# Expert rows gathered as two 4 KB halves from two tables, each half refilled by its own reader

## The chip, the cores and the metric

The kernel runs on one core of a Trainium2 chip. The metric is the device time of one execution in microseconds, the median of several runs. One profiled execution supplies the trace.

## The reference, cut to what matters

The model is a two-layer transformer-like block followed by a second block. The change touches only the last stage of the second block, a product-key expert layer over 256 tokens in two blocks of 128. For each token and each of 8 heads, 16 of 16384 experts are selected; an expert has a row of `u_tab` and a row of `v_tab`, each 1024 float32 (4 KB):

```
eidx = take_along_axis(cidx, pos)                       # 128 tokens x 8 heads x 16 experts
gates = softmax(best)
act = gelu(einsum('td,thkd->thk', hb, u_tab[eidx]))     # dot of each token with its expert's u row
out = einsum('thk,thkd->td', gates * act, v_tab[eidx])  # weighted sum of the v rows
```

So 2 x 8 x 16 = 256 steps each take one u row and one v row for each of 128 tokens.

## The kernel before, in words

The stage is the function `peer` (from L3004). Tokens lie on the 128 partitions. A step `e` (0 to 255) handles one of the 16 experts of one of the 8 heads of one token block; a unit is the 16 steps of one head, so there are 16 units.

The host packs each expert's u row and v row side by side in one table `experts` of 8 KB rows. GpSimd (POOL) issues one indirect DMA a step (L3164), which fetches one 8 KB row for each partition, 1 MB in all, into slot `e % 8` of a ring of 8 slots (`fetched`, L3039). Four slots lie in the `work` buffer and four in `weight_ring`, which is why each operation of the trace has two names. `urows` and `vrows` (L3040) are the two halves of a slot.

What a step does, by engine:

- POOL waits until the slot is free and issues the gather. The first four need no slot wait; those of steps 4 to 7 wait for the query products that used `weight_ring`; from step 8 on POOL waits for `product`, PE's count of finished steps (L3161). At the first step of each unit it waits also for `ranked` (L3159), the count of units whose expert numbers are found.
- VectorE (DVE) waits for the gather's semaphore and multiplies the u half by the tokens with a running sum (L3187). It writes the product back over the u half, and counts `vec_out`. Between the steps it does a slice of the search for later units' experts (the class `Search`: L3066 to L3140).
- ScalarE (ACT) applies Gelu (L3276), multiplies by the gate (L3278), and scales an identity matrix by the result (L3282), which it counts in `act_out`.
- PE waits for `act_out` and for the gather, and runs two 512-column products of that diagonal matrix with the v half, accumulated in PSUM (L3382). Its last one counts `product`. In the first four units PE also runs a query product (L3319) in each step.

POOL's instructions run in program order, so a wait holds everything behind it. All 256 gathers are issued by POOL and run on one queue, q0 in the trace. SP issues four loads of query weights at the start and two stores at the ends of the token blocks.

Of the kernel before, what the change touches and what calls it, by code (L numbers as in the profile page):

```python
# [51 lines left out]
PEER_RING = 8  # L52
# [60 lines left out]
class Core:  # L113


    def __init__(self, nc, ctx):
# [24 lines left out]
        def sem(name):  # L141
            return ctx.enter_context(nc.semaphore(name))
# [136 lines left out]
        self.fetched = False  # L279

        self.gathered = [sem(f"gathered{i}") for i in range(PEER_RING)]

        self.constants_loaded = sem("constants_loaded")
        self.rows_loaded = sem("rows_loaded")
# [2719 lines left out]
def peer(c, a, out_rows):  # L3004
# [10 lines left out]
    experts_u = experts.bitcast(U32)  # L3015
# [136 lines left out]
    with c.stage() as block:  # L3152
        units = [(u, u // H) for u in range(2 * H)]

        @block.gpsimd
        def _(pool):
            for e in range(2 * H * K):
                if e % K == 0:
                    pool.wait_ge(c.ranked, e // K + 1)  # L3159
                if e >= R:  # L3160
                    pool.wait_ge(c.product, e - R + 1)  # L3161
                elif e >= R // 2:
                    pool.wait_ge(c.queried, e - R // 2 + 1)
                pool.indirect_dma_start(  # L3164
                    out=fetched[e % R], out_offset=None, in_=a["experts"],
                    in_offset=bass.IndirectOffsetOnAxis(ap=experts_u[:, e:e + 1], axis=0)
                ).then_inc(c.gathered[e % R], 16)

        @block.vector
        def _(dve):  # L3170
# [135 lines left out]
        @block.tensor  # L3306
        def _(pe):
            def weights(n):
                if n < len(PEER_EARLY):
                    pe.wait_ge(c.ahead[n], 16 * had[n])  # L3310
                    return c.ring[:, n]
                pe.wait_ge(c.late_loaded[n - len(PEER_EARLY)], 16)
                return late_slots[n - len(PEER_EARLY)]

            def query_product(n, i, k):

                if i == 0 and k == 0 and n >= 2:
                    pe.wait_ge(c.query_copied, n - 1)
                last = pe.matmul(query_bank(n)[:, i * NLAT:(i + 1) * NLAT], weights(n)[:, k, i * P:(i + 1) * P], hs[:, k, :],  # L3319
                                 start=k == 0, stop=k == KT - 1)  # L3320
                if i == 1 and k == KT - 1:
                    last.then_inc(c.queried, 1)

            def query(n):
                for i in range(2):
                    for k in range(KT):
                        query_product(n, i, k)

            def score(n):
                pe.wait_ge(c.query_copied, n + 1)  # L3330
                if n == 0:
                    pe.wait_ge(c.side_loaded, 16)
                if n >= 2:
                    pe.wait_ge(c.score_copied, n - 1)
                for t in range(2):
                    for i in range(2):
                        last = pe.matmul(score_bank(n)[:, (2 * t + i) * P:(2 * t + i + 1) * P],  # L3337
                                         qh[:, 2 * queried[n] + i, t * P:(t + 1) * P], keys[:, i, :], start=True, stop=True)
                last.then_inc(c.scored, 1)

            def turn_tokens(t):
                for r in (2 * t, 2 * t + 1):
                    for i in range(4):
                        k = 4 * (r % 2) + i
                        last = pe.transpose(c.banks[r][:, i * P:(i + 1) * P], hs[:, k, t * P:(t + 1) * P], c.constant("ident"))  # L3345
                    last.then_inc(c.token_turned, 1)

            def turn_rows(n):

                if n == 0:  # L3350
                    pe.wait_ge(c.score_copied, 2 * H // 2)
                if n >= 4:
                    pe.wait_ge(c.row_copied, n - 3)
                for i in range(4):
                    k = 4 * (n % 2) + i
                    if n < 4:
                        source = c.x[:, k, NCTX + n // 2 * P:NCTX + (n // 2 + 1) * P]
                    else:
                        column = c.mod[:, 5 * KT + k, 0:1] if n < 6 else c.vector("final_norm", k, k + 1)
                        source = column.to_broadcast([P, P])  # L3360
                    last = pe.transpose(c.banks[4 + n % 4][:, i * P:(i + 1) * P], source, c.constant("ident"))  # L3361
                last.then_inc(c.row_turned, 1)

            query(0)
            turn_tokens(0)
            score(0)
            turn_tokens(1)
            query(1)
            query(2)
            score(1)  # L3370
            query(3)
            score(2)
            score(3)
            pe.wait_ge(c.token_copied, 4)

            for u, t in units:
                for at in range(K):
                    e, r = u * K + at, at % R
                    pe.wait_ge(c.act_out, e + 1)
                    pe.wait_ge(c.gathered[r], 16 * (e // R + 1))  # L3380
                    for half in range(2):
                        last = pe.matmul(c.banks[2 * t + half][:], diag[:, r, :], vrows[r][:, half * 512:(half + 1) * 512],  # L3382
                                         start=e == t * H * K, stop=e == (t + 1) * H * K - 1)
                    last.then_inc(c.product, 1)
                    if u < len(PEER_LATE):
                        query_product(len(PEER_EARLY) + u, at // KT, at % KT)
                    if 0 <= u - 1 < len(PEER_LATE) and at == 5:
                        score(len(PEER_EARLY) + u - 1)
                    if u == PEER_ROWS_UNIT and at < 8:
                        turn_rows(at)  # L3390
# [20 lines left out]
STREAMED = ("w_in", "w_br_ml", "w_br_da", "w_br_fn", "w_out", "w_ffn_in", "w_ffn_out", "w_in_2", "w_out_2",  # L3411
            "s5_glu_w_2", "peer_wq_2")

PACKED = ("vectors", "lambdas", "w_ada_first", "condition_rows", "ada_turned", "constants", "residual", "s5_b", "s5_c", "s5_bt", "s5_rows", "keys", "experts")
OUT = (NLAT, D)


# [91 lines left out]
def pack_inputs(x):  # L3509
    tokens = np.concatenate([x["ctx"][0], x["x"][0]], 0)  # L3510
    m = {name: np.ascontiguousarray(x[name]) for name in STREAMED}
    by_slot = np.arange(D).reshape(FN_GROUPS, FN_C)
    by_slot = np.concatenate([by_slot[:, 0:P + 1], by_slot[:, :P:-1]], 1).reshape(-1)
    m["w_br_fn"] = np.ascontiguousarray(x["w_br_fn"][:, by_slot, :])
    m["vectors"] = pack_vectors(x)
    m["lambdas"] = np.ascontiguousarray(np.broadcast_to(x["da_lam"].reshape(1, -1), (P, 2 * 4 * DA_DH)))
    m["w_ada_first"] = np.ascontiguousarray(x["w_ada"][0][:, 0:START_TILES * P].reshape(KT, P, -1, CHUNK).transpose(2, 1, 0, 3))
    m["condition_rows"] = np.ascontiguousarray(np.stack([x["c_ctx"].reshape(-1), x["c"].reshape(-1), x["c_2"].reshape(-1)]))
    wide = np.stack([x["w_ada"][0], x["w_ada"][1], x["ada_w_2"][0]])
    m["ada_turned"] = np.ascontiguousarray(wide.reshape(3, D, 48, P).transpose(0, 3, 2, 1))  # L3520
    m["constants"] = pack_constants()
    m["residual"] = np.ascontiguousarray(tokens.T.reshape(KT, P, T).transpose(1, 0, 2))

    b = np.zeros((2, P, 4, P), np.float32)
    cc = np.zeros((2, P, S5_TILES, 2 * S5_H), np.float32)
    bt = np.zeros((2, P, S5_TILES, 2 * S5_H), np.float32)
    for part, (bn, cn) in enumerate((("s5_b_re_2", "s5_c_re_2"), ("s5_b_im_2", "s5_c_im_2"))):
        for g in range(S5_G):
            i, second = g // 2, g % 2
            row = 2 * S5_H * (i % 4) + S5_H * second  # L3530
            b[part, row:row + S5_H, i // 4, S5_P * second:S5_P * (second + 1)] = x[bn][0, g].T
            tile = S5_ORDER.index(i)
            cc[part, S5_P * second:S5_P * (second + 1), tile, S5_H * second:S5_H * (second + 1)] = x[cn][0, g].T
            bt[part, S5_P * second:S5_P * (second + 1), tile, S5_H * second:S5_H * (second + 1)] = x[bn][0, g]
    m["s5_b"], m["s5_c"], m["s5_bt"] = b.transpose(1, 0, 2, 3).reshape(P, 4, 2 * P).copy(), cc, bt
    by_tile = np.stack([value.reshape(4, 4, P) for _, value in s5_parameters(x)])
    m["s5_rows"] = np.ascontiguousarray(np.repeat(by_tile.transpose(0, 2, 1, 3), 2 * S5_H, 1).reshape(3, P, 4 * P))
    m["experts"] = np.concatenate([x["peer_u_2"][0], x["peer_v_2"][0]], 1)
    m["keys"] = np.ascontiguousarray(np.stack([x["peer_keys1_2"][0].T, x["peer_keys2_2"][0].T], 1))
    return m  # L3540

# [14 lines left out]
```

## Time and profile before

| What | Value |
|---|---|
| median of 3 runs | 3282.04 us (3276.58 to 3290.23) |
| profiled execution | 3289.03 us |
| its span, first to last instruction | 3287.2 us |
| mean granted TensorE clock | 0.983 |
| PE, DVE, ACT, POOL busy, share of the span | 93%, 50%, 23%, 10% |
| queue q0 (issued by POOL) | 51936 packets, 343.17 MB |

The shares are averages over all stages. The expert stage is the last fifth of the span. "Idle before" in a row is the time that the engine stood before those instructions, with what ended it; a DMA-issuing instruction of POOL is shown with the time that it took to write its descriptors, not with the transfer's.

### The profile page before, as it was taken

Reading aid. Unit: us, or ns where it says so; the run is one execution under the profiler, and the core shown is the slowest. Engines: PE = TensorE matmul, PEld = TensorE weight load, DVE = VectorE, ACT = ScalarE, POOL = GpSimd, SP = SyncE. Lnnn points to the kernel's source line nnn. Section 1 sums busy time; section 2 is a strip of 40 time slices with the busy share of each in tenths; the row PEclk is TensorE's granted clock in tenths of the full one; section 3 lists DMA queues with packets and bytes.
Section 4 is the critical chain, followed back from the end, with each engine's and each line's share of the span. In section 5 each row is a group of like instructions: output and inputs, shape, how many; then the busy total and the mean of one; then the engine's idle time right before and its main releaser. Section 6 shows DMA issues by size and latency. Waiting matters only on the chain. (4 is left out here: it accounts for less than half of the span.)

```text
span 3287.2 us, 33311 instructions
## 1 busy us (share of the span) xinstructions
PE 3066.1 (93%) x12426; PEld 2126.5 (65%) x12426; DVE 1657.1 (50%) x3666; ACT 766.9 (23%) x1785; POOL 335.8 (10%) x371
## 2 busy tenths in 40 slices
PE   6999999999999999999999999999989899877776
PEld 2556556758888888486776678878877744322222
DVE  4333444356773666313234457553037377777774
ACT  2122133321002100012112330010023244444443
POOL 0000000000000000100000000000000144444432
PEclk9999999999999999999999999999988999999999
DMA  6211111144441544642222234577331599999997
GB/s 233 84 62 60 52 52 52 54 145 135 127 131 63 156 152 131 203 146 78 90 81 73 62 102 154 189 279 268 128 122 53 169 417 420 421 420 421 420 420 305
DMA packets 280767, 585.87 MB, mean 178 GB/s; under 512 B 11736, under 2 KB 231768, under 8 KB 244256
## 3 DMA queue, kind: packets, MB, share of 16 engines
q0 software_dynamic: 51936, 343.17, 26.5%
q1 hardware_dynamic: 228672, 240.58, 22.7%
q8 instruction: 100, 1.64, 0.2%
q14 instruction: 59, 0.48, 0.0%
HBM read 582.63 MB, written 1.08 MB: 178 GB/s over the span
## 5 line engine op out<-in xcount | busy, mean ns | idle before, releaser
L782 PE MATMUL banks<-normed,weight_ring 128*128 128x512 f32 (+1 forms) x1280 | 484.1, 533 | 18.4 <-PEq L308 18.4
L782 PEld LDWEIGHTS banks<-normed,weight_ring 128*128 128x128 f32 x1280 | 243.0, 191 | 238.1 <-issue 227.1
L791 PE MATMUL banks<-weight_ring,normed 128*128 128x256 f32 x1408 | 321.5, 384 | 0.2 <-DVE work L1274 0.2
L3382 PE MATMUL banks<-weight_ring,work 128*128 128x512 f32 x512 | 250.0, 615 | 59.1 <-ACT work L3282 58.1
L3382 PE MATMUL banks<-work 128*128 128x512 f32 x512 | 253.4, 618 | 53.6 <-ACT work L3282 49.7
L791 PEld LDWEIGHTS banks<-weight_ring,normed 128*128 128x128 f32 x1408 | 266.4, 191 | 55.6 <-issue 20.0
L417 DVE CUSTOM_DVE_ANT_0 work<-work 128x1024 f32<-128x1024 f32 x188 | 223.2, 1223 | 125.9 <-DMA work<-ada_turned 107.1
L2046 PE MATMUL banks<-normed,weight_ring 128*128 128x256 f32 x1088 | 242.7, 386 | 11.6 <-DMA weight_ring<-w_ffn_in 5.0
L2046 PEld LDWEIGHTS banks<-normed,weight_ring 128*128 128x128 f32 x1088 | 210.7, 194 | 43.1 <-DMA weight_ring<-w_ffn_in 6.3
L3382 PEld LDWEIGHTS banks<-weight_ring,work 128*128 128x128 f32 x512 | 89.0, 190 | 199.2 <-ACT work L3282 133.9
L3382 PEld LDWEIGHTS banks<-work 128*128 128x128 f32 x512 | 88.6, 190 | 197.8 <-ACT work L3282 131.9
L1583 PE MATMUL banks<-branches,weight_ring 128*128 128x256 f32 (+1 forms) x656 | 207.5, 478 | 3.4 <-PEq L308 3.4
L3187 DVE CUSTOM_DVE_ANT_0 work<-work,branches 128x1024 f32<-128x1024 f32 x128 | 156.8, 1225 | 96.3 <-DMA work<-experts,branches 96.0
L3187 DVE CUSTOM_DVE_ANT_0 weight_ring<-weight_ring,branches 128x1024 f32<-128x1024 f32 x128 | 156.8, 1225 | 89.1 <-DMA weight_ring<-experts,branches 87.4
L1583 PEld LDWEIGHTS banks<-branches,weight_ring 128*128 128x128 f32 x656 | 124.6, 190 | 84.6 <-issue 75.5
L1607 PE MATMUL banks<-work 128*128 128x256 f32 x744 | 165.6, 379 | 0.0
L3164 POOL DMA_INDIRECT work<-experts,branches x128 | 135.0, 1055 | 243.8 <-PE banks L3382 171.4
L2046 PE MATMUL banks<-branches,weight_ring 128*128 128x256 f32 x736 | 159.8, 379 | 0.0
L3164 POOL DMA_INDIRECT weight_ring<-experts,branches x128 | 140.0, 1094 | 181.6 <-PE banks L3382 175.0
L1607 PEld LDWEIGHTS banks<-work 128*128 128x128 f32 x744 | 141.4, 190 | 19.2
L2046 PEld LDWEIGHTS banks<-branches,weight_ring 128*128 128x128 f32 x736 | 139.8, 190 | 19.0
L388 POOL DMA_DIRECT2D work<-ada_turned x98 | 51.8, 529 | 768.3 <-DVEq L423 768.3
(492 smaller groups left out, 3929.5 us busy)
## 6 DMA issues: line engine op xcount, KB each, us to landing
weight_ring<-w_in SPq DMA_DIRECT2D x98, 1024.0 KB, 5.2
weight_ring<-w_ffn_in SPq DMA_DIRECT2D x44, 1024.0 KB, 5.2
work<-ada_turned POOLq DMA_DIRECT2D x80, 512.0 KB, 3.8
work<-ada_turned POOLq DMA_DIRECT2D x18, 1536.0 KB, 9.1
weight_ring<-w_ffn_out SPq DMA_DIRECT2D x20, 1024.0 KB, 5.1
weight_ring<-w_out SPq DMA_DIRECT2D x12, 1024.0 KB, 5.2
weight_ring<-w_br_ml SPq DMA_DIRECT2D x8, 1024.0 KB, 5.2
weight_ring<-w_br_da SPq DMA_DIRECT2D x8, 1024.0 KB, 5.2
```

The source lines that it names most:

```text
L388: pool.dma_start(self.slots[n % ADA_SLOTS][:, 0:nt, :], self.a["ada_turned"][which, :, t0:t0 + nt, :]).then_inc(c.ada_loaded[n % ADA_SLOTS ...
L417: last = dve.tensor_tensor_reduce(out=out, in0=slot[:, t, :], in1=self.rows[:, row, :], scale=1.0, scalar=0.0, op0=ALU.mult, op1=ALU.add, ...
L782: last = pe.matmul(proj_bank(tile)[:, since:T], w[:, kk, half * P:(half + 1) * P], c.h[:, kk, since:T], start=kk == 0, stop=kk == KT - 1)
L791: last = pe.matmul(proj_bank(tile)[:, x * CHUNK:(x + 1) * CHUNK], c.h[:, kk, j * P:(j + 1) * P], w[:, kk, :], start=kk == 0, stop=kk == KT ...
L1583: ins = pe.matmul(bank(i)[:, cols(p0, p1)], w[:, k - at, half * P:(half + 1) * P], source[:, k, cols(p0, p1)], start=k == 0, stop=k == tot ...
L1607: last = pe.matmul(out[:, half * NCTX:(half + 1) * NCTX], left(k), right(k), start=k == 0, stop=k == KT // 2 - 1)
L2046: ins = pe.matmul(bank(i)[:, 0:NLAT], w[:, k - at, half * P:(half + 1) * P], source[:, k, lat], start=k == 0, stop=k == total - 1)
L3164: pool.indirect_dma_start(out=fetched[e % R], out_offset=None, in_=a["experts"], in_offset=bass.IndirectOffsetOnAxis(ap=experts_u[:, e:e + ...
L3187: dve.tensor_tensor_reduce(out=urows[e % R], in0=urows[e % R], in1=tokens[:, t, :], scale=1.0, scalar=0.0, op0=ALU.mult, op1=ALU.add, accu ...
L3382: last = pe.matmul(c.banks[2 * t + half][:], diag[:, r, :], vrows[r][:, half * 512:(half + 1) * 512], start=e == t * H * K, stop=e == (t + ...
```

## The change

The table is split in two, `experts_in` (u rows) and `experts_out` (v rows), with 4 KB rows. A step now has two gathers of 128 rows of 4 KB, 0.5 MB each, with semaphores of their own. The u gather waits for `vec_out`: DVE is done with the u half of the step 8 before. The v gather behind it waits for `product`: PE is done with that step's v half. DVE waits for the first semaphore, PE for the second. Slots, ring depth, DVE's, ACT's and PE's instructions stay.

```diff
         self.gathered = [sem(f"gathered{i}") for i in range(PEER_RING)]
+        self.gathered_out = [sem(f"gathered_out{i}") for i in range(PEER_RING)]
...
                 if e >= R:
-                    pool.wait_ge(c.product, e - R + 1)
+                    pool.wait_ge(c.vec_out, e - R + 1)
                 elif e >= R // 2:
                     pool.wait_ge(c.queried, e - R // 2 + 1)
                 pool.indirect_dma_start(
-                    out=fetched[e % R], out_offset=None, in_=a["experts"],
+                    out=urows[e % R], out_offset=None, in_=a["experts_in"],
                     in_offset=bass.IndirectOffsetOnAxis(ap=experts_u[:, e:e + 1], axis=0)
                 ).then_inc(c.gathered[e % R], 16)
+                if e >= R:
+                    pool.wait_ge(c.product, e - R + 1)
+                pool.indirect_dma_start(
+                    out=vrows[e % R], out_offset=None, in_=a["experts_out"],
+                    in_offset=bass.IndirectOffsetOnAxis(ap=experts_u[:, e:e + 1], axis=0)
+                ).then_inc(c.gathered_out[e % R], 16)
...
                     pe.wait_ge(c.act_out, e + 1)
-                    pe.wait_ge(c.gathered[r], 16 * (e // R + 1))
+                    pe.wait_ge(c.gathered_out[r], 16 * (e // R + 1))
...
-    m["experts"] = np.concatenate([x["peer_u_2"][0], x["peer_v_2"][0]], 1)
+    m["experts_in"] = np.ascontiguousarray(x["peer_u_2"][0])
+    m["experts_out"] = np.ascontiguousarray(x["peer_v_2"][0])
```

## Rows read from the trace of the kernel before

**Rows 1.** Busy time and count by engine, granted clock, DMA share, GB/s, by stretch.

```profile
core 0: us, PE busy (x) PEld busy (x) DVE busy (x) ACT busy (x) POOL busy (x), PEclk, DMA share, GB/s
2600.00:2700.00 100.00, 95.73 (x345) 61.58 (x344) 70.91 (x208) 40.09 (x106) 42.40 (x36) 0.98 0.91 363
2900.00:3000.00 100.00, 76.40 (x157) 26.60 (x156) 74.47 (x186) 44.43 (x128) 42.09 (x39) 1.00 1.01 421
2619.40:3267.40 648.00, 536.87 (x1272) 219.22 (x1271) 452.43 (x1148) 286.46 (x833) 275.07 (x256) 0.99 1.00 415
```

**Rows 2.** The chain that ended last, its last pieces: start us, us, what.

```profile
3236.02 15.21 DMA weight_ring<-experts,branches
...
3255.90 16.17 DMA weight_ring<-experts,branches
...
3274.49 2.00 PE banks L3382 x4
```

**Rows 3.** DMA queues from 2800 to 3200 us: packets, MB, share.

```profile
q0 software_dynamic: 22993, 167.45, 100.8%
q1 hardware_dynamic: 144, 0.52, 0.3%
```

**Rows 4.** POOL in order of time at the stage's start: start us, us, instruction, idle before.

```profile
2619.41 1.01 POOL L3164 DMA_INDIRECT work<-experts,branches  x1 [63.07 <-DVEq L3131]
2620.73 0.95 POOL L3164 DMA_INDIRECT work<-experts,branches  x1 [0.30 <-issue]
...
2625.72 0.94 POOL L3164 DMA_INDIRECT weight_ring<-experts,branches  x1 [0.30 <-issue]
2626.97 0.93 POOL L3164 DMA_INDIRECT weight_ring<-experts,branches  x1 [0.31 <-issue]
```

**Rows 5.** The gathers' line alone: minimum, median, maximum ns; first and last start.

```profile
L3164 POOL DMA_INDIRECT work<-experts,branches x128: 932/936/1967, 2619.4 to 3245.9; - x128
L3164 POOL DMA_INDIRECT weight_ring<-experts,branches x128: 932/937/1991, 2624.5 to 3255.9; - x128
```

**Rows 6.** Groups by line, from 2600 us on: count, busy us, mean ns, idle before.

```profile
L3187 DVE CUSTOM_DVE_ANT_0 work<-work,branches 128x1024 f32<-128x1024 f32 x128 | 156.8, 1225 | 96.3 <-DMA work<-experts,branches 96.0 <-DVE work L3114 0.2
L3164 POOL DMA_INDIRECT weight_ring<-experts,branches x128 | 140.0, 1094 | 181.6 <-PE banks L3382 175.0 <-issue 4.0 <-PE banks L3319 2.7
L3164 POOL DMA_INDIRECT work<-experts,branches x128 | 135.0, 1055 | 243.8 <-PE banks L3382 171.4 <-DVEq L3131 63.1 <-issue 9.4
```

**Rows 7.** DVE, POOL and others in order of time, around 2886 and 2907 us.

```profile
2886.24 1.23 DVE L3187 CUSTOM_DVE_ANT_0 weight_ring<-weight_ring,branches 128x1024 f32<-128x1024 f32 x1 [1.24 <-DMA weight_ring<-experts,branches]
2886.37 1.91 POOL L3164 DMA_INDIRECT weight_ring<-experts,branches  x1 [0.57 <-PE banks L3382]
2887.40 0.08 DVE L3187 DVE_READ_ACCUMULATOR2_ANT work<- 128x1 f32 x1
...
2906.73 0.94 POOL L3164 DMA_INDIRECT weight_ring<-experts,branches  x1 [1.59 <-PE banks L3382]
2907.14 1.22 DVE L3187 CUSTOM_DVE_ANT_0 weight_ring<-weight_ring,branches 128x1024 f32<-128x1024 f32 x1 [0.86 <-DMA weight_ring<-experts,branches]
```

**Rows 8.** DMA issues: count, KB each, median us from issue to landing.

```profile
work<-ada_turned POOLq DMA_DIRECT2D x80, 512.0 KB, 3.8
work<-ada_turned POOLq DMA_DIRECT2D x18, 1536.0 KB, 9.1
```

**Rows 9.** The line that issues those loads: minimum, median, maximum ns.

```profile
L388 POOL DMA_DIRECT2D work<-ada_turned x98: 528/528/567, 2.0 to 2247.3; - x98
```

**Rows 10.** The DMA view from 2600 to 2610 us: only loads with 1 KB rows.

```profile
DMA packets 3496, 3.53 MB, mean 353 GB/s; under 512 B 48, under 2 KB 3496, under 8 KB 3496
q1 hardware_dynamic: 3496, 3.53, 109.3%
```

**Rows 11.** Around the last step, in order of time.

```profile
3272.20 1.23 DVE L3187 CUSTOM_DVE_ANT_0 weight_ring<-weight_ring,branches 128x1024 f32<-128x1024 f32 x1 [1.25 <-DMA weight_ring<-experts,branches]
...
3274.49 1.98 PE L3382 MATMUL banks<-weight_ring,work 128*128 128x512 f32 x4 [0.50 <-ACT work L3282]
```

More of the change, by code:

```diff
@@ L3412 @@
             "s5_glu_w_2", "peer_wq_2")
-PACKED = ("vectors", "lambdas", "w_ada_first", "condition_rows", "ada_turned", "constants", "residual", "s5_b", "s5_c", "s5_bt", "s5_rows", "keys", "experts")
+PACKED = ("vectors", "lambdas", "w_ada_first", "condition_rows", "ada_turned", "constants", "residual", "s5_b", "s5_c", "s5_bt", "s5_rows", "keys", "experts_in", "experts_out")
 OUT = (NLAT, D)
```

## The prediction

> **What bounds the kernel now.** I read the stretches first. In the expert stage the DMA share is 1.01 at 421 GB/s, while PE is busy 76 us of 100, DVE 74 and POOL 42 [rows 1]. The chain of waits agrees: its last fifth is made of gathers of 15 to 16 us each with a few microseconds of compute between them, down to the last gather, issued at 3255.90 and landed at 3272.07 [rows 2]. A gather that needs 15 us stands in line behind six others. The queue view says the same: q0 alone takes 100.8% of the 16 engines' time [rows 3]. So a step costs what 1 MB costs on the DMA engines: 1.0486 MB / 421 GB/s = 2.49 us, and 256 steps 638 us of the 648 us between the first issue and the end of the transfers [rows 1]. PE (two products) and DVE (one L3187 of 1.225 us [rows 6] and a slice of search) both wait in each step. POOL has one gather a step and spends the rest waiting for PE: of its idle time before gathers, 175.0 + 171.4 us were ended by PE's products [rows 6].
>
> **What the change takes away.** It lets the u half be refilled when DVE is done with it instead of when PE is, about 3 to 4 us earlier (DVE's end at 3273.4 and PE's at 3276.5 in the last step [rows 11]). With the DMA engines full, an earlier request only waits longer in the queue: the bytes are the same, so this is worth nothing in the steady state. It is also partly undone by POOL's order, since the u gather stands behind the previous step's v gather and its wait for `product`. At the end something is won: the last u half lands one half gather (1.24 us, below) before the last v half, so DVE and ACT (3272.20 to 3274.49 [rows 11]) run partly beside that transfer. Gain 1.2 us.
>
> **What it adds on POOL.** 256 more gathers, 512 in all. The price of one is its descriptor writing, 0.936 us in the median [rows 5], plus 0.30 us to the next where nothing is waited for [rows 4]. Together 1.24 us, and the starts 2625.72 and 2626.97, with a satisfied wait between them, show the same 1.25. Does a row of half the length make it cheaper? Direct loads from POOL come with 4 KB rows (512 KB) and 12 KB rows (1536 KB) [rows 8], and all 98 take 528 to 567 ns [rows 9]. So the row count sets it, and 128 rows stay 128 rows. Bounds: 0.47 us (half of the median) if it went by bytes, 0.94 if by rows; I take 0.94. A step then needs 2 x 1.24 = 2.48 us of POOL against 2.49 us of DMA. POOL, which had half its time free, has none left.
>
> **The second term: starts that are held back.** The mean of a gather is not 0.936 but (140.0 + 135.0)/256 = 1.074 us [rows 6]. Where the excess comes from is seen at 2886.37: that gather began inside DVE's L3187, took 1.91 us, and ended 0.9 us after L3187's end at 2887.40, as if it had started only then; the one at 2906.73 began 0.4 us before L3187 and took 0.94 [rows 7]. So a gather that starts inside L3187 is held until it ends. Before, that cost nothing, since POOL had slack and its starts followed PE's end, mostly outside L3187. Now POOL is never idle and each step of two starts contains one L3187. Bounds per gather: 0, if the starts settle in the free part (2.49 - 1.16 = 1.33 us free, 1.24 needed, 0.09 us of play); 0.30 us, if they fall at random (1.2 of 2.49 us occupied, 0.6 us mean rest: 0.49 x 0.61). I take the measured mean, 1.074 - 0.936 = 0.138 us, which lies between. For 512 gathers: 512 x 0.138 = 71 us. This is 0.28 us a step, and a step is 2.76 us: POOL takes the place of the DMA engines as the bound. A free cross-check: if a held u gather starts at L3187's end, and L3187 follows the u gather's issue by 4.3 us, two steps last 4.3 + 1.16 = 5.46 us, 2.73 us each.
>
> The Trainium skill speaks against this term. "DMA: Bandwidth & Descriptors" (Anatomy of one DMA) calls descriptor generation small, and says that many descriptors can be emitted before it shows. By that rule POOL would cost nothing and the sum would be the first rival's. The trace disagrees: 0.94 us for 128 rows at a spacing of 1.25.
>
> **What it adds on the DMA engines.** Twice the packets, and 16 more semaphore writes a step. No loads with 4 KB rows alone are in the trace. Below: nothing, or a gain if short packets overlap better, at most a few us, since 421 GB/s at a share of 1.01 leaves no gap. Above: loads with 1 KB rows run at 353 GB/s when alone [rows 10], 2.97 us for 1 MB against 2.49. That is 0.48 us for 7 x as many added packets as the change adds; one doubling is 0.069 us a step, 17.5 us in all. I take 17.5 us as the DMA engines' own cost, and 0 in the sum: 2.56 us a step is below POOL's 2.76, which hides it. If POOL's holding is less than 0.07 us a step, this decides.
>
> The same page (Why small descriptors are slow) gives a fixed overhead of about three cycles for each packet. An estimate from it, at its 850 MHz, is 3.5 ns x 8 packets x 256 = 7 us; by it the DMA-bound rival would come out about 10 us lower.
>
> **The sum.** POOL starts at 2619.41 as before [rows 4], and nothing stops it: steps 0 to 7 take it to 2619.4 + 16 x 1.24 = 2639.2, when the first products are done (PE freed slot 0 by 2639.06, the first POOL start that waited for it). Later its waits for `vec_out` and `product` are met long before: from issue to the end of PE's step is 4.2 (landing) + 2.3 (DVE and ACT) + 2.0 (PE) = 8.5 us, three steps of the ring's eight. The last gather starts at 2619.4 + 511 x 1.239 + 71 = 3323.5. It lands 4.2 us later: 3.8 for the 512 KB load [rows 8] and 0.4 for the longer descriptor writing; no line stands before it any more. 3327.7 against 3272.07 is +55.6, less 1.2 at the end: +54.4. The profiled execution took 3289.03, so its like would take 3343; it lay 7 us above the median of the runs, so the median is 3282 + 54 = 3336 us. What follows the last product is unchanged. The clock stays: it is granted at 1.00 with PE busy 76 of 100 us [rows 1], and at 2.76 us a step PE is busy 70.
>
> **Rivals.**
> 1. POOL falls into step and hides: its starts settle in the free 1.33 us after each L3187, and the DMA engines stay the bound at 2.49 us. For it: in the steady state most gathers of before show 936 ns, and DVE's rhythm follows the transfers. Against it: 0.09 us of play, and search slices of varied length before each L3187. It decides below 0.01 us of holding a step. Time: 3282 - 1.2 = 3281, not slower.
> 2. The same, but shorter packets cost the 17.5 us: 3282 + 17.5 - 1.2 = 3298.
> 3. Starts fall at random: a step is p with 1.225/p of it occupied, two starts held 0.61 us each: p = 2.48 + 1.5/p, p = 2.98. Holding is 0.50 x 256 = 128 us: 3282 + 128 - 71 + 54 = 3393. For it: in steps with long search slices DVE's start wanders. Against it: a held start is set to L3187's end, which puts the next one 1.24 us later in the free part.
> 4. The change does not do what it says (POOL's order holds the u refill): true in part, and worth nothing either way, as the refill is early enough.
> 5. Faster: gathers of 4 KB rows run above 421 GB/s and descriptor writing goes by bytes. Removing all of the share's 1% and more, 3% of 638 us, gives 3263. Nothing in the rows speaks for it.
>
> **How the numbers follow.** Forecast (POOL bound, holding 0.15 to 0.42 us a step, 3304 to 3371) 0.55, at 3336; random starts 0.17; DMA-bound with packet cost 0.10; hidden 0.14; faster 0.04. A measurement tells about 0.5%, 16 us, from no change. Slower: 0.55 + 0.17 + half of 0.10 = 0.77; same: 0.14 + 0.05 = 0.19; faster 0.04. The range takes in rival 2 and rival 3: 3286 to 3396. The forecast's own range is 3304 to 3371.
>
> **What the profile of the changed kernel would show.** POOL: x512 gathers, busy over 85% of the stage, mean ns above 1000 with a median still near 936, idle before them ended by "issue" and almost never by PE. DMA share in the stage near 0.92 and 380 GB/s; landing 4 to 6 us instead of 15. Q0 packets up by 32768 + 4096. Starts of DVE's L3187 2.76 us apart. I am wrong if the DMA share stays at 1.0 and landing stays at 8 us or more (rivals 1 and 2, told apart by GB/s: 421 or 410), if the median gather is near 0.5 us (POOL's price goes by bytes), or if POOL's idle time is ended by PE (the ring, not POOL, is short).

## The result and the profile after

The changed kernel takes 3344.14 us (median of 4 runs, 3337.87 to 3351.53) against 3281.76 us for the kernel before: 1.9% slower, ratio 1.0185 with a 95% interval of 1.0163 to 1.0207. The prediction was 3336 us, in a range of 3286 to 3396.

The stretches, in the columns of [rows 1]; the last covers nearly the whole expert stage:

```profile
2900.00:3000.00 100.00, 69.95 (x143) 24.06 (x141) 66.74 (x174) 38.68 (x116) 78.37 (x72) 1.00 0.99 372
3100.00:3200.00 100.00, 69.14 (x140) 23.79 (x140) 62.27 (x161) 36.82 (x111) 78.68 (x71) 1.00 0.99 367
2619.40:3320.00 700.60, 537.07 (x1234) 212.04 (x1233) 451.37 (x1139) 284.80 (x832) 544.12 (x505) 0.99 1.00 381
```

POOL is busy 78 us of 100 and not 42. Its busy time leaves out the 0.30 us between two gathers: 72 x 0.30 = 22 us, which makes the 100. The bytes come at 372 GB/s instead of 421. The DMA share, however, still reads 0.99. The groups of POOL and DVE, which answer to [rows 6] (count, busy us, mean ns, idle before):

```profile
L3194 DVE CUSTOM_DVE_ANT_0 work<-work,branches 128x1024 f32<-128x1024 f32 x128 | 156.8, 1225 | 130.7 <-DMA work<-experts_in,branches 128.0 <-ACT work L3289 2.3 <-DVE work L3115 0.2
L3171 POOL DMA_INDIRECT weight_ring<-experts_out,branches x128 | 146.4, 1144 | 39.0 <-issue 38.7 <-PE banks L3389 0.3
L3171 POOL DMA_INDIRECT work<-experts_out,branches x128 | 143.7, 1123 | 39.0 <-issue 37.8 <-PE banks L3389 1.2
L3165 POOL DMA_INDIRECT weight_ring<-experts_in,branches x128 | 131.5, 1028 | 39.0 <-issue 39.0
L3165 POOL DMA_INDIRECT work<-experts_in,branches x128 | 129.2, 1009 | 101.9 <-DVEq L3132 63.2 <-issue 38.7
```

The sum is 550.8 us for 512 gathers, a mean of 1.076 us; before it was 1.074. The waits on PE, 346 us before [rows 6], are down to 1.5; behind the first gather's wait for the expert numbers (63.2 us, as before), 0.30 us of "issue" ahead of each gather is all that is left. The DMA view from 2800 to 3200 us, to set against [rows 3]:

```profile
DMA packets 41530, 151.35 MB, mean 378 GB/s; under 512 B 4614, under 2 KB 4614, under 8 KB 41511
q0 software_dynamic: 41367, 150.62, 99.1%
weight_ring<-experts_in,branches POOLq DMA_INDIRECT x71, 6.4
```

A gather lands 6.4 us after its issue; in [rows 2] it was 15 to 16. The rate is not even: in the same view's slices of 10 us it runs from 346 to 412 GB/s. The chain of waits, whose last fifth was DMA before, now names POOL, gather after gather (start us, us, what):

```profile
2890.24 1.41 POOL weight_ring L3165
2891.65 0.30 issue
2891.96 1.80 POOL weight_ring L3171
2893.75 0.30 issue
2894.06 0.94 POOL work L3165
2895.00 0.30 issue
```

And two held starts in order of time, as in [rows 7]. The second gather begins inside DVE's L3194 (2899.83 to 2900.99) and ends at 2901.88, 0.89 us after it (a gather alone takes 0.94 in all):

```profile
2899.16 0.94 POOL L3165 DMA_INDIRECT work<-experts_in,branches  x1 [0.30 <-issue]
2899.83 1.23 DVE L3194 CUSTOM_DVE_ANT_0 work<-work,branches 128x1024 f32<-128x1024 f32 x1 [1.06 <-DMA work<-experts_in,branches]
2900.41 1.47 POOL L3171 DMA_INDIRECT work<-experts_out,branches  x1 [0.30 <-issue]
2900.99 0.08 DVE L3194 DVE_READ_ACCUMULATOR2_ANT work<- 128x1 f32 x1
2902.18 0.94 POOL L3165 DMA_INDIRECT work<-experts_in,branches  x1 [0.30 <-issue]
```

The start times in the whole trace show how regular this is. Of the 512 gathers 253 start while a dot product runs (68 of 256 before), and each of these ends some 0.8 us after the dot product's row ends, or takes its usual 0.94 us where it started in the last 0.13 us. 147 of the 253 start in the dot product's last 0.25 us and are held for little.

First and last steps (start of the first gather, the last two gathers, the last dot product and the last product):

```profile
2610.86 1.01 POOL L3165 DMA_INDIRECT work<-experts_in,branches  x1 [63.23 <-DVEq L3132]
...
3315.14 0.95 POOL L3165 DMA_INDIRECT weight_ring<-experts_in,branches  x1 [0.30 <-issue]
3316.40 0.94 POOL L3171 DMA_INDIRECT weight_ring<-experts_out,branches  x1 [0.30 <-issue]
3321.72 1.23 DVE L3194 CUSTOM_DVE_ANT_0 weight_ring<-weight_ring,branches 128x1024 f32<-128x1024 f32 x1 [1.33 <-DMA weight_ring<-experts_in,branches]
3324.00 1.98 PE L3389 MATMUL banks<-weight_ring,work 128*128 128x512 f32 x4 [0.58 <-ACT work L3289]
```

From the first gather to the start of the last product it is 713.1 us (3324.00 - 2610.86) against 655.1 before (3274.49 - 2619.41): +58.0. The stages ahead of it, which the change does not touch, were 8.5 us shorter in this execution, so the spans differ by only 49.5 us. The medians differ by 62.

### The profile page after: what moved, and what is told of

Read it like the earlier page. It is cut to its first block and busy times, and to the rows that moved or that the text cites. A ratio compares the mean times of both kernels' runs of the same rounds, so it can differ in the third digit from the quotient of the medians.

```text
span 3336.7 us, 33567 instructions
## 1 busy us (share of the span) xinstructions
PE 3061.0 (92%) x12426; PEld 2119.0 (64%) x12426; DVE 1656.6 (50%) x3666; ACT 767.2 (23%) x1785; POOL 611.8 (18%) x627
## 5 line engine op out<-in xcount | busy, mean ns | idle before, releaser
L3194 DVE CUSTOM_DVE_ANT_0 work<-work,branches 128x1024 f32<-128x1024 f32 x128 | 156.8, 1225 | 130.7 <-DMA work<-experts_in,branches 128.0
L3194 DVE CUSTOM_DVE_ANT_0 weight_ring<-weight_ring,branches 128x1024 f32<-128x1024 f32 x128 | 156.8, 1225 | 112.7 <-DMA weight_ring<-experts_in,branches 111.9
L3171 POOL DMA_INDIRECT weight_ring<-experts_out,branches x128 | 146.4, 1144 | 39.0 <-issue 38.7
```

The source lines that it names most:

```text
L3171: pool.indirect_dma_start(out=vrows[e % R], out_offset=None, in_=a["experts_out"], in_offset=bass.IndirectOffsetOnAxis(ap=experts_u[:, e:e ...
L3194: dve.tensor_tensor_reduce(out=urows[e % R], in0=urows[e % R], in1=tokens[:, t, :], scale=1.0, scalar=0.0, op0=ALU.mult, op1=ALU.add, accu ...
```

## The experiments

Two theories. **POOL**: the issuing engine sets the step, with 2 x 1.24 us plus 0.28 us of held starts; the DMA engines would need only some 2.56 us. **Packets**: the DMA engines are still the bound, as their share of 0.99 says, and 4 KB packets give them only 378 GB/s. Each kernel below ran beside the kernel before, in two groups. Its median was 3285.78 us beside one wait put back, tokens in PSUM on the changed kernel, direct v loads and 64-row gathers, and 3286.36 us beside the other four.

### One wait put back

```diff
                 if e >= R:
-                    pool.wait_ge(c.vec_out, e - R + 1)
+                    pool.wait_ge(c.product, e - R + 1)
```

> The changed kernel with one wait put back: the u gather waits for PE's product, as before the change. POOL theory (POOL's descriptor writing plus the starts held by DVE's L3187 set the step at 2.75 us, and the waits are met long before): no difference from the changed kernel, 3344 us within 10, idle time before gathers ended by issue. Rival (the earlier refill is worth something, and the loss would be larger without it): some 3360 us or more, with POOL's idle time ended by PE.

Measured: 3347.69 us (3336.83 to 3359.09), ratio 1.0181 (1.0144 to 1.0218), beside 1.0185 for the changed kernel. One of its groups, which still stands before its gathers for "issue" and hardly for PE:

```profile
L3165 POOL DMA_INDIRECT weight_ring<-experts_in,branches x128 | 134.4, 1050 | 39.0 <-issue 38.1 <-PE banks L3389 0.9
```

The earlier refill of the u half is worth nothing that can be measured.

### The changed kernel with DVE's tokens in PSUM

```diff
-                    dve.tensor_tensor_reduce(out=urows[e % R], in0=urows[e % R], in1=tokens[:, t, :], scale=1.0,
+                    dve.tensor_tensor_reduce(out=urows[e % R], in0=urows[e % R], in1=c.psum[:, (2, 6)[t]:(4, 8)[t], :].rearrange("p b n -> p (b n)"), scale=1.0,
...
-            copy_tokens(0)
...
-            copy_tokens(1)
...
+                    if u == PEER_ROWS_UNIT + 1 and at == 0:
+                        pe.wait_ge(c.row_copied, 8)
+                        turn_tokens(1)
```

> The changed kernel with the tokens read by DVE from PSUM, so that the dot product has one operand in SBUF and not two (the copies of the tokens to SBUF fall away). Holding theory: a gather that starts inside the dot product is no longer held, the mean gather falls from 1.076 us to below 1.0, a step from 2.75 to 2.48 to 2.56 us, the time by 50 to 70 us to 3275 to 3295. Rival (the DMA engines bound the changed kernel, since their share still is 0.99 to 1.01 there, and 4 KB packets give only 378 GB/s): the gathers get shorter but the time stays within 10 us of 3344.

The two copies of the tokens to SBUF fall away, and PE turns the second block's tokens later, in the seventh unit.

Measured: 3304.98 us (3297.87 to 3308.63), ratio 1.0069 (1.0044 to 1.0094). The loss falls from 62 to 19 us. The groups of this kernel, columns as above:

```profile
L3194 DVE CUSTOM_DVE_ANT_0 work<-work,banks 128x1024 f32<-128x1024 f32 x128 | 156.3, 1221 | 105.3 <-DMA work<-experts_in,branches 105.0 <-DVE work L3115 0.2
L3165 POOL DMA_INDIRECT weight_ring<-experts_in,branches x128 | 120.8, 944 | 39.0 <-issue 33.8 <-DVE work L3194 4.9 <-PE banks L3321 0.3
L3171 POOL DMA_INDIRECT weight_ring<-experts_out,branches x128 | 120.2, 939 | 50.7 <-issue 28.8 <-PE banks L3382 21.9
```

A stretch of it:

```profile
2900.00:3000.00 100.00, 74.30 (x153) 25.81 (x152) 71.78 (x180) 43.51 (x125) 72.16 (x77) 1.00 1.03 410
```

The dot product is as long as before (1221 ns), and 244 of the 512 gathers start while it runs, nearly as many as the 253 of the changed kernel. Yet none of the 244 takes over 1.03 us, and the mean of all is 0.94. In order of time:

```profile
2900.65 1.22 DVE L3194 CUSTOM_DVE_ANT_0 weight_ring<-weight_ring,banks 128x1024 f32<-128x1024 f32 x1 [1.51 <-DMA weight_ring<-experts_in,branches]
2901.05 0.93 POOL L3165 DMA_INDIRECT weight_ring<-experts_in,branches  x1 [0.30 <-issue]
```

This gather begins 0.40 us into the dot product and takes 0.93 us. So the held starts are real and come from the dot product's second operand in SBUF: with it in PSUM they go. The Trainium skill has a rule for this in "SBUF — State Buffer" (Who interferes with whom): a DVE instruction with two SBUF inputs contends with a GpSimd instruction that reads SBUF. The runs agree: of the 253 gathers that start inside the dot product with two SBUF inputs none ends sooner than 0.8 us after it, and of the 244 inside the one with a single SBUF input none takes over 1.03 us. The same section of the Trainium skill infers that descriptor generation is not stalled by such a DVE instruction, since it needs the write side alone. For these gathers the runs show otherwise. What a gather reads from SBUF at its start is taken to be the expert numbers; no run separates that. The theory of packets is refuted: with unchanged packets the rate went from 378 to 409 GB/s. With the holds gone the engines change places once more: POOL has waits on PE again, landing is back at 17 us (weight_ring<-experts_in, 16.9), and the DMA engines bound the step at 1.0486 MB / 409 GB/s = 2.56 us, which is 19 us in 256 steps above the 2.49 of 8 KB packets.

### One gather a step, all packets of 4 KB

```diff
-                if e >= R:
-                    pool.wait_ge(c.product, e - R + 1)
-                pool.indirect_dma_start(
-                    out=vrows[e % R], out_offset=None, in_=a["experts_out"],
...
+                sp.dma_start(vrows[e % R], a["experts_out"][e * 60:e * 60 + P]).then_inc(c.gathered_out[e % R], 16)
```

> The changed kernel, but the v half is a direct load of 128 consecutive 4 KB rows issued by SP, not a gather (it leaves out the choice of the v rows; the expert numbers are used for the u rows alone). POOL has one gather a step, all packets stay at 4 KB, bytes stay. POOL theory: the DMA engines are the bound again at 410 to 421 GB/s, 3278 to 3300 us; POOL is busy 40 to 45% of the stage. Rival (4 KB packets cost the time): 378 GB/s and 3335 to 3350 us.

The kernel leaves out the choice of the v rows: SP loads 128 neighbouring rows.

Measured: 3298.89 us (3293.71 to 3309.73), ratio 1.0044 (1.0026 to 1.0063). DMA view from 2800 to 3200 us:

```profile
DMA packets 44907, 163.67 MB, mean 409 GB/s; under 512 B 4986, under 2 KB 4986, under 8 KB 44887
```

The packets are as in the changed kernel, POOL has half its gathers, and the loss is 0.4% instead of 1.9%. The rate, 409 GB/s, is the one of the run before, so it is what 4 KB packets give in this stage when POOL does not limit.

### Two gathers a step, the long packets kept

```diff
                 ).then_inc(c.gathered[e % R], 16)
+                pool.indirect_dma_start(
+                    out=extra[:, e % R, :], out_offset=None, in_=a["tiny"],
+                    in_offset=bass.IndirectOffsetOnAxis(ap=experts_u[:, e:e + 1], axis=0)
+                ).then_inc(c.gathered[e % R], 16)
...
-                    dve.wait_ge(c.gathered[e % R], 16 * (e // R + 1))
+                    dve.wait_ge(c.gathered[e % R], 32 * (e // R + 1))
```

> The kernel before (one gather of 8 KB rows a step), with a second gather of 128 rows of 64 bytes behind each into a scratch that nobody reads. 512 gathers as in the changed kernel, but the 1 MB of a step still moves in 8 KB packets. POOL theory: twice 1.24 us and the held starts set a step at about 2.75 us, 3335 to 3350 us, DMA at 380 GB/s or so. Rival (the changed kernel's loss is its short data packets): the time stays near 3286, or at most as far up as 8 small packets an engine cost (one doubling of packets cost 0.07 us a step, 18 us in all: 3304).

Measured: 3341.57 us (3340.02 to 3349.49), ratio 1.0171 (1.0154 to 1.0189). Two of its three groups of gathers:

```profile
L3168 POOL DMA_INDIRECT work<-tiny,branches x256 | 290.8, 1136 | 78.1 <-issue 78.1
L3164 POOL DMA_INDIRECT work<-experts,branches x128 | 127.1, 993 | 101.3 <-DVEq L3131 62.5 <-issue 37.2 <-PE banks L3386 1.5
```

The queue of the gathers from 2800 to 3200 us, and their landing:

```profile
q0 software_dynamic: 25571, 153.64, 99.3%
weight_ring<-experts,branches POOLq DMA_INDIRECT x72, 5.6
```

The 1 MB of a step is fetched just as before the change, and 64 bytes for each row beside it cost 55 of the 62 us. What costs is the second descriptor-writing instruction, not the shape of the transfer; and since the 256 gathers of 64-byte rows take at least 945 ns each, its price does not go by bytes. It also settles the DMA share: 99.3% at 386 GB/s, with landing in 5.6 us, in a kernel whose POOL waits on PE for 1.8 us in all.

### Half of the steps split

```diff
+def SPLIT(e):
+    return e % 2 == 0
...
+                if SPLIT(e):
+                    for out, table, landed in ((urows, "experts_in", c.gathered), (vrows, "experts_out", c.gathered_out)):
+                        pool.indirect_dma_start(
+                            out=out[e % R], out_offset=None, in_=a[table],
+                            in_offset=bass.IndirectOffsetOnAxis(ap=experts_u[:, e:e + 1], axis=0)
+                        ).then_inc(landed[e % R], 16)
+                    continue
...
+                    if SPLIT(e):
+                        pe.wait_ge(c.gathered_out[r], 16 * (e // R + 1))
```

> The kernel before, but every second step is split into a u gather and a v gather of 4 KB rows from tables of their own, as in the change (both behind the old wait). 384 gathers. POOL theory: 1.5 x 1.24 + held starts = 2.07 us a step, below the DMA engines', so only half of the packet cost is paid: 3286 + 9 = 3295 us, POOL's idle time ended by PE. Rival (each added gather costs its share of the loss): half of 60 us, 3315.

Measured: 3296.57 us (3286.57 to 3303.22), ratio 1.0025 (1.0013 to 1.0038): +8 to +10 us, not the half of the loss. Four of its six groups of gathers have waits on PE, this one the most:

```profile
L3171 POOL DMA_INDIRECT weight_ring<-experts_in,branches x64 | 79.3, 1239 | 44.8 <-PE banks L3396 33.8 <-issue 11.0
```

The holds came to more than I took (mean gather 1.25 us; 1.5 x 1.55 = 2.3 us a step), but still below the DMA engines' 2.53, so they cost nothing; the 8 to 10 us fit half of the packets' 19. The price of a gather more on POOL is a threshold and not a slope.

### The kernel before with 64-row gathers

```diff
-                pool.indirect_dma_start(
-                    out=fetched[e % R], out_offset=None, in_=a["experts"],
-                    in_offset=bass.IndirectOffsetOnAxis(ap=experts_u[:, e:e + 1], axis=0)
-                ).then_inc(c.gathered[e % R], 16)
+                for lo in (0, 64):
+                    pool.indirect_dma_start(
+                        out=fetched[e % R][lo:lo + 64], out_offset=None, in_=a["experts"],
+                        in_offset=bass.IndirectOffsetOnAxis(ap=experts_u[0:64, e:e + 1], axis=0)
+                    ).then_inc(c.gathered[e % R], 16)
```

> The kernel before, but each step's gather of 128 rows of 8 KB is two gathers of 64 rows each (both halves of the partitions use the first 64 tokens' expert numbers, so the second half of the choice is left out). 512 gathers, but the same packets and bytes as before. If descriptor writing goes by rows (0.5 to 0.6 us each and 0.30 between): POOL needs 1.7 us a step and hides, 3282 us within 10. If it goes by instruction (0.94 us each): a step is 2.7 us as in the changed kernel, some 3340 us, though packets are 8 KB long.

The kernel leaves out the second half of the choice: both halves of the partitions fetch the same 64 experts.

Measured: 3757.95 us, which neither theory expected. The four runs lie far apart (3622.14 to 3801.91), and the trace is of the slowest; even the fastest lost over 330 us. The line of the gathers (minimum, median, maximum ns):

```profile
L3165 POOL DMA_INDIRECT work<-experts,branches x256: 883/889/1942, 2615.1 to 3743.9; - x128
```

And a stretch:

```profile
2900.00:3000.00 100.00, 62.53 (x109) 22.50 (x108) 39.33 (x99) 23.85 (x72) 40.54 (x44) 0.78 1.02 230
```

The question that it was made for is answered: 64 rows take 889 ns against 936 for 128, so the price hardly goes by rows; it goes nearly all by the instruction. The time comes from elsewhere: POOL waits on PE again (541 us over its 512 gathers), a gather lands 29 us after its issue, and the DMA engines are at 1.02 with 230 GB/s, a little over half of 421. Each of these gathers writes to half of the partitions, and the two halves also fetch the same rows; no run separates the two. In this stretch the mean granted clock was 0.78, with PE busy 63 of 100 us.

### The kernel before with the tokens in PSUM

```diff
-                    dve.tensor_tensor_reduce(out=urows[e % R], in0=urows[e % R], in1=tokens[:, t, :], scale=1.0,
+                    dve.tensor_tensor_reduce(out=urows[e % R], in0=urows[e % R], in1=c.psum[:, (2, 6)[t]:(4, 8)[t], :].rearrange("p b n -> p (b n)"), scale=1.0,
...
```

> The kernel before, with the tokens read by DVE from PSUM as in the experiment on the changed kernel. Starts of gathers are no longer held (mean 0.94 us and not 1.07), but POOL had slack and the DMA engines are the bound: no difference, 3286 us within 5. Rival (held starts cost the kernel before too): 3270 or less.

Measured: 3288.23 us (3278.53 to 3290.32), ratio 0.9998 (0.9989 to 1.0007). The gathers' mean fell to 0.94 us, and the time did not move:

```profile
L3164 POOL DMA_INDIRECT weight_ring<-experts,branches x128 | 120.6, 943 | 200.1 <-PE banks L3375 197.4 <-PE banks L3314 1.8 <-issue 0.9
```

The 35 us of holds (256 x 0.138) cost the kernel before nothing. In the changed kernel they have doubled to 71 us and POOL is the bound; taking them away won 43 us (62 - 19), down to where the DMA engines bound it again.

### A try at a faster version

The tokens in PSUM, their transposes behind the first score, and only the last two steps split:

```diff
+def SPLIT(e):
+    return e >= 254
...
+            score(0)
             turn_tokens(0)
-            score(0)
-            turn_tokens(1)
```

> A try at a version that beats both: the kernel before with the tokens in PSUM, PE's transposes of them moved behind the first score product, and only the last two steps split into u and v gathers. Gains: the first gather 0.9 us earlier, and at the end the last v half beside DVE and ACT, 1.2 us. 3283 us against 3286, below what the runs can tell; the trace should show the first gather earlier and PE starting the last step within 0.5 us of its v half's landing.

Measured: 3286.17 us (3276.09 to 3290.23), ratio 0.9999 (0.9989 to 1.0009). No faster version came of it. The gain at the end can be seen in the profiled execution, in the last dot product and the start of the end phase after the last product:

```profile
3259.31 1.22 DVE L3199 CUSTOM_DVE_ANT_0 weight_ring<-weight_ring,banks 128x1024 f32<-128x1024 f32 x1 [1.32 <-DMA weight_ring<-experts_in,branches]
...
3263.61 1.29 DVE L3212 TENSOR_TENSOR work<-banks,branches 128x512 f32<-128x512 f32 x2 [3.07 <-PE banks L3389]
```

From the first gather (2607.95) to that instruction it is 655.7 us, and 657.1 before (3276.51 - 2619.41): 1.4 us won where 1.2 was expected. The kernel before with the tokens in PSUM, which splits no step, took 657.8 us for it. These are single executions, so the size is rough. The 0.9 us at the start cannot be read, since the stages ahead vary by more from run to run, and the interval of the ratio is 3 us wide to each side.

## Why the prediction was right

- **The bound changes engines.** Right. The idle time of POOL is ended by "issue". The run with one gather a step loses 13 us and the one whose second gather moves almost nothing loses 55, so the count of gathers and not the transfer sets the time.
- **1.24 us a gather.** Right to 1%: 0.94 plus 0.30. The reason given, that the row count sets it, was wrong. It rested on rows in which the row length varied and the row count did not; at 64 rows it is 889 ns. So what the prediction quotes from the Trainium skill ("DMA: Bandwidth & Descriptors", Anatomy of one DMA) is half borne out: more descriptors in one gather cost little, 47 ns for 64 rows more, but writing them is not small, since nearly all of the 0.94 us stays whatever their number.
- **Held starts, 71 us for 512.** Right: 550.8 us of POOL time is 512 x 0.936 + 71.6. The forecast from first to last gather start was 511 x 1.239 + 71 = 704.1 us; measured 705.5 (3316.40 - 2610.86). That the mean hold stayed at 0.14 us was in part luck: it depends on how starts fall against the dot product, and with every other step split it was 0.31 us. The rival of random starts had the share right (0.49 taken, 253 of 512 measured) and the rest wrong: 71.6 us over 253 starts is 0.28 us each and not 0.61, since more than half of them fall in the dot product's last 0.25 us. The cross-check of two steps in 5.46 us agreed by chance, as it took 4.3 us from a u gather's issue to its dot product; in the last step it was 6.6 (3315.14 to 3321.72).
- **Packets, 2.56 us a step, hidden.** Right in size, 409 GB/s and 2.56 us in two kernels, where DMA was the bound; hidden in the changed kernel as a whole, though not in each stretch: its best slices, 408 to 412 GB/s, are at that rate.
- **Landing in 4.2 us, DMA share 0.92.** Both wrong. Landing takes 6.4 us (2.2 us more than taken), and the share stays at 0.99 at 372 GB/s. The first was taken from a load issued into nearly idle queues, with nothing standing before it. But where no start is held, POOL needs 2.48 us a step and the DMA engines 2.56, so a short line forms: the last four dot products start 2.55 us apart (3314.06 to 3321.72), the DMA engines' pace. That this line is the whole of the 2.2 us is inferred. The second assumed that packets keep their duration when fewer wait. Of my signs of failure, "DMA share stays at 1.0" alone would have misled; with the landing time it did not hold.
- **The end, 1.2 us won.** In the changed kernel it is not seen as such: the last product waits for ACT, that is for the u half's landing, and the v half is there in time. By the sum the last product starts 5.4 us after the last gather (4.2 of landing, 2.4 of DVE and ACT, less the 1.2 won); it started 7.6 us after it (3324.00 - 3316.40). The forecast for the stage in the profiled execution, +54.4, falls 3.6 us short of +58.0: 1.4 us by the starts of the gathers, 2.2 by the landing.
- **The earlier refill.** Worth nothing, as said; one wait put back shows it.

## What to carry to other kernels

Before a transfer is split, multiply the issuing engine's spacing (here 1.24 us a gather, whatever is in it) by the new count and set it against the bytes' time. Slack on that engine is a threshold: below it another gather cost no more than its packets, above it each costs its full price, holds included. A buffer freed earlier was worth nothing here, where the issuing engine was the bound and its waits were long met; whether it helps where a queue runs empty no run here shows.

## What the runs showed of the hardware

- A gather that starts inside a DVE instruction with two operands in SBUF is held to its end (253 of 512 started so, 106 of 512 took over 1.1 us); with one operand in PSUM the mean is 0.94 us, and DVE's instruction is no longer for it (1221 against 1225 ns).
- An indirect gather costs POOL 889 ns for 64 rows and 936 for 128, plus 0.30 us, and no less for rows of 64 bytes (945 ns at least) than for rows of 8 KB.
- The DMA share read 0.99 at 372 to 386 GB/s where POOL was the bound, and 1.00 to 1.03 at 409 to 421 where it was not: it hardly tells a full queue from one fed just in time. Landing time does: 5.6 to 6.4 us for a step's gathers against 14 to 19.
- Gathers that write 64 partitions moved 230 GB/s, those that write 128 moved 421, both with rows of 8 KB; the cause is open.
